# Two transformer layers on one core: a fourth raw place in the down-projections, GpSimd's splits moved, norm turns placed later

## The reference, cut to what matters

```python
x = x + concat([tok, xa], axis=-1) @ w_out          # mixer: gated linear attention (layer 0), dilated attention (layer 1)
x = x + conv_ffn(rms_norm(x, ffn_norm), w_up, conv_w, conv_b, w_down)

def conv_ffn(h, w_up, conv_w, conv_b, w_down):
    u = causal_dwconv(h @ w_up, conv_w, conv_b)      # 1024 x 5632, 3 taps
    gate, val = split(u, 2, axis=-1)
    return (silu(gate) * val) @ w_down               # (1024 x 2816) @ (2816 x 1024)
```

## Time and profile before

| | before |
|---|---|
| median of three runs | 2499.7 us |
| the profiled execution | 2497.09 us |
| its span | 2495.3 us |
| TensorE busy | 2423.2 us, 97% |
| VectorE busy | 1731.1 us, 69% |
| ScalarE busy | 1033.1 us, 41% |
| GpSimd busy | 226.0 us, 9% |
| mean granted TensorE clock | 0.992 |

### The profile page before, as it was taken

One profiled execution on the slowest core, in us unless ns is written; L12 is line 12 of the kernel. 1 busy time (PEld: TensorE's weight loads), 2 busy tenths in 40 slices (PEclk: granted clock), 3 DMA queues, 4 the chain that ended last, 5 costly groups with the idle time before them and its releaser, 6 DMA issues. The chain is left out here.

```text
span 2495.3 us, 32379 instructions
## 1 busy us (share of the span) xinstructions
PE 2423.2 (97%) x11700; PEld 2049.3 (82%) x11700; DVE 1731.1 (69%) x2908; ACT 1033.1 (41%) x2126; POOL 226.0 (9%) x271
## 2 busy tenths in 40 slices
PE   7999999999999999998999999999999999999998
PEld 7998877888888887877899889887788888888777
DVE  4432584489999988985544562463769998998996
ACT  6433553344444444445325332333335444443443
POOL 1010030000000000052212122122000000000000
PEclk9999999999999999999999999999999999999999
DMA  4231122222222247742202111212532222226864
GB/s 150 84 96 22 39 80 77 76 69 93 85 76 93 85 166 275 250 160 81 68 1 82 35 35 47 56 34 82 170 115 68 93 85 77 87 82 224 289 199 145
DMA packets 207542, 257.72 MB, mean 103 GB/s; under 512 B 38377, under 2 KB 141785, under 8 KB 207385
## 3 DMA queue, kind: packets, MB, share of 16 engines
q1 hardware_dynamic: 203224, 255.65, 31.3%
q10 hardware_dynamic: 4160, 0.02, 0.1%
HBM read 206.54 MB, written 49.09 MB: 102 GB/s over the span
## 5 line engine op out<-in xcount | busy, mean ns | idle before, releaser
L52 PE MATMUL psum<-f_T_lo 128*128 128x512 f32 x616 | 243.6, 396 | 11.4 <-DVE f_T_lo L676 10.3
L53 PE MATMUL psum<-f_T_lo 128*128 128x512 f32 x616 | 240.7, 391 | 0.0
L54 PE MATMUL psum<-f_T_lo 128*128 128x512 f32 x616 | 240.6, 391 | 0.0
L52 PE MATMUL psum<-w_hi,hT_hi 128*128 128x512 f32 x576 | 230.0, 399 | 4.2 <-DVE w_lo L1445 2.5
L54 PE MATMUL psum<-w_hi,hT_lo 128*128 128x512 f32 x576 | 226.9, 394 | 0.0
L53 PE MATMUL psum<-w_lo,hT_hi 128*128 128x512 f32 x576 | 226.9, 394 | 0.0
L52 PEld LDWEIGHTS psum<-f_T_lo 128*128 128x128 f32 x616 | 116.0, 188 | 45.8 <-DVE f_T_lo L676 18.9
L52 PEld LDWEIGHTS psum<-w_hi,hT_hi 128*128 128x128 f32 x576 | 125.2, 217 | 22.6 <-issue 3.9
L54 PEld LDWEIGHTS psum<-w_hi,hT_lo 128*128 128x128 f32 x576 | 125.5, 218 | 18.0
L53 PEld LDWEIGHTS psum<-w_lo,hT_hi 128*128 128x128 f32 x576 | 125.5, 218 | 16.7
L52 PE MATMUL psum<-hT_hi,f_up_hi 128*128 128x512 f32 x352 | 137.4, 390 | 0.4 <-DVE f_up_lo L615 0.4
(11 more groups left out here) (416 smaller groups left out, 6076.1 us busy)
## 6 DMA issues: line engine op xcount, KB each, us to landing
raw<-in_ffn_w_up_dram SPq DMA_DIRECT2D x88, 512.0 KB, 4.7
activations<-f_act SPq DMA_DIRECT2D x44, 512.0 KB, 2.6
f_up_pieces<-activations SPq DMA_DIRECT2D x38, 512.0 KB, 4.3
w_raw<-in_b_w_in_dram SPq DMA_DIRECT2D x18, 1024.0 KB, 6.0
f_up_pieces<-in_ffn_w_down_dram SPq DMA_DIRECT2D x20, 512.0 KB, 4.9
x_between<-XY SPq DMA_DIRECT2D x16, 512.0 KB, 5.3
XY<-x_between SPq DMA_DIRECT2D x16, 512.0 KB, 6.2
f_up_pieces<-activations SPq DMA_DIRECT2D x28, 256.0 KB, 3.9
```

The lines of the kernel that those rows point to most:

```text
L52: nc.tensor.matmul(out, lhs_hi, rhs_hi, start=start, stop=False)
L53: nc.tensor.matmul(out, lhs_hi, rhs_lo, start=False, stop=False)
L54: return nc.tensor.matmul(out, lhs_lo, rhs_hi, start=False, stop=stop)
```

## The change

The down-projections get a fourth raw place, used by `n % 4`: rooms of the same kind, two tiles of `X` for group 13 and the two activation tiles from group 17. A load waits for the low parts of group n-4; the load of group 3 waits for product P4 and mix U4 of the last up-projection unit. The loads of rows 0 to 3 of `X` move to groups 18 to 21, and the last store of activations moves by one group. In group 22 (`n == 2 * PAIRS`) product 1 comes ahead of product 0.

In step 3 of `f0` the turns of tiles 0 to 2 stand behind groups 4, 5 and 7, and that of tile 3 between the banks of the tail; ScalarE's and VectorE's parts of the norm are placed to fit. VectorE makes the two low parts of the begun weights there, in place of GpSimd in step 2. In the begun block's group 1 the turns of tiles 0 to 2 stand behind all matmuls of tiles 4 and 5.

In the last attention GpSimd's chunks 3 to 5 wait until the first tile is merged (`added`), and `load_second` is issued one tile earlier. The functions `raw_pair`, `raw_single` and `raw_odd` give the places; `raw_odd` changes in the same manner as `raw_pair` and isn't shown.

```diff
-        act_out = [sb(f"act{i}", [P, SEQ]) for i in range(2)]
+        act_room = sb("act", [P, 2, SEQ])
+        act_out = [act_room[:, i, :] for i in range(2)]
...
-        r_loaded, e_loaded = ([sem(f"{n}_loaded{s}") for s in range(k)] for n, k in (("r", 3), ("e", 4)))
+        r_loaded, e_loaded = ([sem(f"{n}_loaded{s}") for s in range(k)] for n, k in (("r", 4), ("e", 4)))
...
         def raw_pair(n, i):
-            if n % 3 == 2:
-                return up.pieces[:, 4 * i:4 * i + 2, :]
+            if n % 4 >= 2:
+                return up.pieces[:, 4 * i + 2 * (n % 2):4 * i + 2 * (n % 2) + 2, :]
             if n < PAIRS:
-                return h_room[1 - n % 3][:, 2 * i:2 * i + 2, SECOND]
-            if n % 3 == 0:
-                return up.pieces[:, 4 * i + 2:4 * i + 4, :]
-            return up.room[:, i, :].rearrange("p (h n) -> p h n", n=HALF)
+                return h_room[1 - n % 4][:, 2 * i:2 * i + 2, SECOND]
+            return raw_room(n)[:, i, :].rearrange("p (h n) -> p h n", n=HALF)
+
+        def raw_room(n):
+            if n % 4 == 0:
+                return up.room[:, :, :]
+            return X[:, 0:2, :] if n == PAIRS + 2 else act_room[:, :, :]
 
         def raw_single(n):
             if n >= LAST:
-                return (up.pieces[:, 2, :], up.pieces[:, 6, :], up.room[:, 0, FIRST], up.pieces[:, 0, :])[(n - LAST) % 4]
-            return p1 if n % 3 == 2 else (sums_a, sums_b)[n % 3].rearrange("p d n -> p (d n)")
+                return up.pieces[:, (0, 4, 2, 6)[(n - LAST) % 4], :]
+            return (sums_a.rearrange("p d n -> p (d n)"), sums_b.rearrange("p d n -> p (d n)"), p1, u2)[n % 4]
...
                 elif n == 2:
                     sp.wait_ge(p_done, product(FC - 1, P2))
                     sp.wait_ge(mixed, mix(FC - 1, C11))
+                elif n == 3:
+                    sp.wait_ge(p_done, product(FC - 1, P4))
+                    sp.wait_ge(mixed, mix(FC - 1, U4))
                 elif n in (PAIRS + 1, PAIRS + 2):
                     sp.wait_ge(p_done, ALL)
                     sp.wait_ge(conv_done, 2 * FC)
-                if n >= 3:
-                    sp.wait_ge(b_split, parts_until(n - 2))
+                elif n == PAIRS + 6:
+                    sp.wait_ge(act_stored, 16 * FC)
+                if n >= 4:
+                    sp.wait_ge(b_split, parts_until(n - 3))
...
-                if n == PAIRS + 1:
+                if n == PAIRS + 2:
                     store_act(FC - 1)
-                if n in (14, 16, 18, 20):
-                    load_rows((n - 14) // 2)
+                if n >= 2 * PAIRS - 4 and n < 2 * PAIRS:
+                    load_rows(n - 2 * PAIRS + 4)
...
-                if norm and g >= 4:
-
-                    if g == 4:
-                        square(0)
-                    if g == 5:
-                        scale(0)
-                        square(1)
-                    if g == 6:
-                        scale(1)
-                        norm.act_high(act, 0)
-                        square(2)
-                    if g == 7:
-                        scale(2)
-                    if g == 8:
-                        norm.act_high(act, 1)
-                        square(3)
-                    if g == 9:
-                        scale(3)
-                    if g == 10:
-                        norm.act_high(act, 2)
+                if norm and g == 4:
+                    square(0)
+                if norm and g == 5:
+                    scale(0)
+                    square(1)
+                if norm and g == 7:
+                    scale(1)
+                if norm and g == 8:
+                    norm.act_high(act, 0)
+                    square(2)
+                if norm and g == 10:
+                    scale(2)
                 high_parts(LAST + g)
             if norm:
-                norm.act_high(act, 3)
+                norm.act_high(act, 1)
+                square(3)
+                norm.act_high(act, 2)
+                scale(3)
                 act.wait_ge(b_split, parts_until(LAST + PAIRS))
                 square(4)
                 square(5)
+                norm.act_high(act, 3)
...
-            for g in range(5, PAIRS):
-                lows(LAST + g)
-                if norm and g in (5, 7, 9):
-                    norm.dve_gain(dve, (g - 5) // 2)
-                elif norm:
-                    norm.dve_low(dve, (g - 6) // 2)
+            lows(LAST + 5)
             if norm:
-                norm.dve_gain(dve, 3)
+                begin_low(0)
+                norm.dve_gain(dve, 0)
+            lows(LAST + 6)
+            lows(LAST + 7)
+            if norm:
+                begin_low(1)
+                norm.dve_gain(dve, 1)
+            lows(LAST + 8)
+            lows(LAST + 9)
+            if norm:
+                norm.dve_low(dve, 0)
+            lows(LAST + 10)
+            if norm:
+                norm.dve_gain(dve, 2)
             for i in range(4):
                 rows_last(i)
+                if norm and i == 0:
+                    norm.dve_low(dve, 1)
                 if norm and i == 1:
-                    norm.dve_low(dve, 3)
+                    norm.dve_gain(dve, 3)
+                    norm.dve_low(dve, 2)
+            if norm:
+                norm.dve_low(dve, 3)
...
             def _(pool):
-                if begin:
-                    begin.low_parts(pool)
                 for t in range(TT):
                     norm.pool(pool, t)
...
-                for which in range(2):
+                for which in (1, 0) if n == 2 * PAIRS else (0, 1):
...
-                if norm and g in (2, 3, 4, 6):
-                    turn_first((2, 3, 4, 6).index(g))
+                if norm and g in (4, 5, 7):
+                    turn_first((4, 5, 7).index(g))
             pe.wait_ge(b_split, parts_until(LAST + PAIRS))
             for i in range(4):
                 for g in range(PAIRS - TAIL, PAIRS):
                     last = group_product(LAST + g, 0, i, False, g == PAIRS - 1)
                 last.then_inc(out_done, 1)
+                if norm and i == 1:
+                    turn_first(3)
...
     def split_ahead(self, pool, merge):
         for k in range(self.ahead):
             if k == self.ahead // 2:
-                pool.wait_ge(merge.weighed, 1)
+                pool.wait_ge(merge.added, 1)
...
-    def low_parts(self, pool):
-        for kh in range(2):
-            pool.wait_ge(self.high, kh + 1)
-            self.nc.gpsimd.tensor_tensor(self.lo[kh], self.raw(kh), self.hi[kh].bitcast(F32), ALU.subtract).then_inc(self.split, 1)
+    def low_part(self, dve, kh):
+        dve.wait_ge(self.high, kh + 1)
+        self.nc.vector.tensor_tensor(self.lo[kh], self.raw(kh), self.hi[kh].bitcast(F32), ALU.subtract).then_inc(self.split, 1)
...
                     live = [t for t in group if b or t >= ready]
+                    late = begun and b == 0 and g == 1
...
-                                if t == live[0]:
+                                if t == live[0] and not late:
                                     turns(before[2:])
...
-                        if kh == 0:
+                        if kh == 0 and not late:
                             turns(before[:2])
+                    if late:
+                        turns(before)
...
-                if merge and t == TT - 2:
+                if merge and t == TT - 3:
                     merge.load_second(sp, ahead.split, ahead.chunks)
```

More of the change, by code:

```diff
@@ L150, in ffn_phase @@
                         [x[:, :].rearrange("p (d n) -> p d n", d=DC) for x in conv_out],
-                        [x[:, :].rearrange("p (d n) -> p d n", d=DC) for x in act_out], sums_room)
+                        [x.rearrange("p (d n) -> p d n", d=DC) for x in act_out], sums_room)
         def product(c, i):
@@ L237, in raw_pair @@
         def raw_pair(n, i):
-            if n % 3 == 2:
-                return up.pieces[:, 4 * i:4 * i + 2, :]
+            if n % 4 >= 2:
+                return up.pieces[:, 4 * i + 2 * (n % 2):4 * i + 2 * (n % 2) + 2, :]
             if n < PAIRS:
-                return h_room[1 - n % 3][:, 2 * i:2 * i + 2, SECOND]
-            if n % 3 == 0:
-                return up.pieces[:, 4 * i + 2:4 * i + 4, :]
-            return up.room[:, i, :].rearrange("p (h n) -> p h n", n=HALF)
+                return h_room[1 - n % 4][:, 2 * i:2 * i + 2, SECOND]
[4 more added lines that the diff above has]
+            return X[:, 0:2, :] if n == PAIRS + 2 else act_room[:, :, :]
         def raw_single(n):
             if n >= LAST:
-                return (up.pieces[:, 2, :], up.pieces[:, 6, :], up.room[:, 0, FIRST], up.pieces[:, 0, :])[(n - LAST) % 4]
-            return p1 if n % 3 == 2 else (sums_a, sums_b)[n % 3].rearrange("p d n -> p (d n)")
+                return up.pieces[:, (0, 4, 2, 6)[(n - LAST) % 4], :]
+            return (sums_a.rearrange("p d n -> p (d n)"), sums_b.rearrange("p d n -> p (d n)"), p1, u2)[n % 4]
         def raw_odd(n):
```

(21 more changed lines are left out.)

## The result

The changed kernel takes 2475.45 us (median of four runs, 2475.02 to 2478.44), the kernel before 2499.69 in the same comparison: ratio 0.9906, 95% interval 0.9889 to 0.9923, 24.2 us less. Forecast were 2475.7 us and 24.0 less.

The account below looks back on a forecast made before the run. The prediction took TensorE, where it stands still or runs slowly, as the bound. Its terms, 4.7 + 3.1 + 0.3 + 3.0 + 3.5 + 1.8 + 7.6 = 24.0, came off 2497.1; with 2.6 added: 2475.7 us, range 2470 to 2486.

Parts of the forecast that it names:

- Four raw places: Down-projections, groups 0 to 11: earlier loads end waits for late activations, gaining 4.7 us in the first layer, 3.1 in the second.
- Products swapped: Group 22: VectorE is itself behind, so only the second sums' earlier start in the first layer counts, 0.3 us.
- GpSimd's splits: Groups 28 to 32: slowed VectorE sums and a late load go, so the 3.0 us lost there come back.
- Last step: Last step of the first down-projection: later turns let the begun tile start earlier, 3.5 us gained if the clock holds.
- The waits of 1.1 and 1.25: Last step: new TensorE waits in us, 1.1 before the tail and 1.25 before the begun tile, for VectorE's low parts.
- against the rival: Rival, chance 0.18: the clock stays low in the last step and begun block, costing 1.7 and about 1.5 us; 2479.
- Begun block: Begun block: 24 matmuls ahead of the first turns fill a wait, and the head-row chain comes 1.8 us earlier.
- Merge: Last attention: 6.6 us back from undisturbed scalings, clock included, and 1.0 from earlier second loads; sum 7.6 us.
- the rival, at the low end of its price: Rival, chance 0.15: chunk 5's load and split end behind the attention, or SP's stores hold ScalarE; price 2 to 6 us.
- one of the signs named for being wrong: End of the last attention: TensorE waiting there would show the forecast wrong; no size given.
- The 1.0 for the second loads: Behind the last attention: TensorE's 1.37 us wait for the merged tile shrinks as second loads go out earlier; 1.0 us.
- The last rival: Rival, chance 0.03: collisions only change victims, GpSimd's splits meeting other scalings; 2496 to 2500 us.

Follow-up runs that it names:

- e1: Changed kernel with three raw places again in both down-projections, row loads and last store moved back too; 2488.9 us, ratio to before 0.9945.
- e5: Changed kernel with product 0 ahead of product 1 in group 22 again; 2477.4 us, ratio to before 0.9891.
- e4: Changed kernel with the begun weights' two low parts made by GpSimd in step 2 again, none by VectorE; 2479.8 us, ratio to before 0.9902.
- e7: Changed kernel with the last step's turns and norm parts as before, and the begun weights' two low parts on GpSimd; 2485.6 us, ratio to before 0.9930.
- e8: Kernel of e3 with the norm's low part 0 later and low part 3 earlier on VectorE in the last step; 2470.6 us, ratio to before 0.9870.
- e6: Changed kernel with the turns of head rows within the matmuls of the begun block's group 1 again; 2475.9 us, ratio to before 0.9895.
- e3: Changed kernel with the load of weight chunk 5 issued behind the store of tile 4, not ahead; 2472.9 us, ratio to before 0.9878.
- e10: Changed kernel with the merge's second loads issued one tile later again, GpSimd's chunks still behind the first merge; 2477.6 us in one run.
- e9: Kernel of e8 with VectorE's 512-column row sums of groups 24 to 27 moved to groups 28 to 31; 2467.4 us, ratio to before 0.9869.
- e2: Changed kernel with both last-attention edits taken back, GpSimd's chunks 3 to 5 and the second loads; 2482.6 us, ratio to before 0.9917.
- after_again: The changed kernel itself, unedited, run once more beside the best version on the same chip; 2476.5 us, ratio to before 0.9901.

## Why the prediction was right, and where it wasn't

The total was right, and mostly for its reasons. From group 0 to the end 23.1 us were gained for the 24.0 worked out: the merge fell short by 2.2, the down-projections' groups 0 to 11 gave 0.7 more, and the stretch up to the last attention gave 0.6 that nobody forecast (it lies between 534.6 and 536.4 in the runs, so it is no effect). The changed stretches alone gave 22.5. That the medians differ by 24.2 and the forecast by 0.25 from the median is closer than the interval, some 4 us to either side, can vouch for: that part is luck.

- *Four raw places* (4.7 and 3.1): right in kind, 5.0 and 3.5 measured. No wait of VectorE for a transfer is left in them, and the rate rose from 269 to 294 GB/s (289 was worked out). e1 shows the cause: the row loads that it moves back as well go out when most of the loss has happened.
- *Products swapped* (0.3): "what group 22 saves, groups 24 to 28 wait" is exact, 0.82 against 0.82 in e5. The 0.3 came out too, by the reason given for it, second sums that start earlier in the first layer because no late load is ahead of them (34.28 us before and after in the second layer). But that is the fourth place's doing and not the swap's, so it stands under the wrong heading.
- *GpSimd's splits* (3.0): 2.9 measured. The late load wasn't needed for the collision: e4 has loads on time and there it costs 4.5. What the Trainium skill states in "GPSIMD Engine Reference", section 8, that GpSimd contends with two-input instructions of VectorE, gave the wrong sum as I had read it (slower for all of the 29 us); what it contends for is told in the last section.
- *Last step* (3.5): 3.4. The waits of 1.1 and 1.25 that were worked out are 1.0 and 1.35, and the clock stayed at 1.00, against the rival. e7 and e8 confirm both sides of it.
- *Begun block* (1.8): 1.9, and here less than half of it is shown to come from what was changed. The turns' place gives 0.8 (e6); the rest goes with the clock. The prediction names the half clock ahead of ScalarE's copy but gives no reason why it should go, and no run shows what moved it.
- *Merge* (7.6): 5.4. The scalings' part was sized right (6.6, measured 6.6 to 7.1). The step that failed is "ScalarE's output for tile 6 waits for that store. I work out 1.1 us late, with two units before TensorE needs it: nothing". The store went out 4.4 us late, not 1.1: 1741.5 where e3 has 1737.1. The rest of the chain then holds as I had written it into the rival, at the low end of its price: 1.9 to 2.9 us. TensorE waiting at the end of the last attention was one of the signs named for being wrong, and it came. The 1.0 for the second loads at the output projection were 1.5, but in the changed kernel they aren't shown to be what brings it: e10, with the loads late and a long end ahead of them, has the short way too.
- *The last rival's price* (2496 to 2500) doesn't follow from its condition: the two terms that hang on collisions are 3.0 and 6.6, and without them the sum gives 2485.3.

## What to carry to other kernels

An engine's queue of transfers has to be followed like an engine: when an edit makes one of its waits end later, put a time to the wait's new end and to each transfer behind it, and move those that are ready ahead of it; three lines did it here. Where VectorE was at its limit in a few groups, reordering TensorE, which reads from it, gave nothing (e5), and moving VectorE's work to groups with room gave all of it (e9). A GpSimd operation isn't harmless because its neighbours on VectorE keep their durations for most of its length: look at its end.

## What was unexpected in the hardware

VectorE and GpSimd shut each other out for whole instructions in these traces. The single durations behind the sums above (ns, least, median and most, first and last start) are, for the scalings of e2, and for GpSimd's two splits and VectorE's two low parts in e4:

```profile
L2767 DVE TENSOR_SCALAR XY<-XY,merge_tops x4: 273/1638/2355, 1730.6 to 1734.0; 128x128 f32<-128x128 f32 x4
```

```profile
L1405 POOL TENSOR_TENSOR f_next_w<-raw,f_next_w x2: 3348/16368/29387, 1055.3 to 1084.6; 128x1024 fp32r<-128x1024 f32 x2
L683 DVE TENSOR_TENSOR f_T_lo<-f_up_pieces,f_T_lo x2: 3385/3404/3423, 1082.3 to 1085.6; 128x1024 fp32r<-128x1024 f32 x2
```

One scaling takes 0.27 us free, and up to 2.36, the length of a split, when one of GpSimd's is under way. In e4 GpSimd's first split begins at 1055.3 and ends at 1084.6, the second takes 3.3; both low parts take 3.4 instead of 1.2, so each was held for 2.2 us, about one split of 2.36. GpSimd's first split must then have waited, not worked, for some 27 us of VectorE's two-input operations, which ran there without a gap. The Trainium skill, "SBUF — State Buffer", section "Who interferes with whom", says this: the shared port pair goes to one instruction as a whole and the other blocks. These rows agree with it in both directions. It also mends my reading of the earlier trace rows: a late load (0.87 idle) was what let GpSimd in there, not a second cost beside it. What let it in in e4 stays open: VectorE's low part at 1082.3 follows the operation ahead of it without idle time.

The last attention's start takes 7.17 us at a clock of 1.00 or 8.72 at 0.80, both in the same kernel (after and after_again), and nothing in between in fourteen traces. The end with its stall has two lengths as well: 9.66 to 9.77 us in four traces (after_again, e4, e5, e6), and 10.49 to 10.77 us in four others (after, e1, e7, e10), where the clock is 0.84. The start doesn't decide which: after_again and e10 both start at 8.7 us, and only in e10 does the clock fall at the end. The stretch ahead of the first down-projection varied by 9 us (917.4 to 926.4) with no edit made there. All three are as large as single terms here, and only distances within one trace could tell 0.8 us apart.
